# Attention of the sample tokens: value products with the probabilities as weights, and the queries' path ahead of the keys

## The chip, the cores and the metric

The kernel runs on one core of one Trainium2 chip. The metric is the device time of one execution in microseconds (us). One core has TensorE (PE, with its weight loads shown apart as PEld), VectorE (DVE), ScalarE (ACT), GpSimd (POOL) and SyncE (SP), each with a queue of its own that is worked off in order, and 16 DMA engines. The engines wait for each other by semaphores.

## The reference

One inference step through two layers, for a prompt of 256 tokens and for 8 sample tokens of 8 sequences, all in float32. Layer 0 has a recurrent branch (a gated linear recurrence over a width-4 convolution) and a differential attention with 4 heads; layer 1 has a gated delta rule and a mixture of 8 experts. The change touches the attention of layer 0:

```python
q = rmsnorm(q.reshape(B, T, H_B, 2, DH_B), g_q)          # H_B = 4, DH_B = 64
k = rmsnorm(k.reshape(B, T, H_B, 2, DH_B), g_k)
s1 = einsum('bqhd,bkhd->bhqk', q1, k1) * DH_B ** -0.5
s2 = einsum('bqhd,bkhd->bhqk', q2, k2) * DH_B ** -0.5
p = softmax(s1) - lam * softmax(s2)
o = einsum('bhqk,bkhe->bqhe', p, v)
o = rmsnorm(o, subln_g) * (1.0 - lam_init)
y = concatenate([gelu(gate) * hs, o]) @ w_out
```

For a sample token, keys and values are 256 rows of its own sequence from a paged cache (2 pages of 128 rows, 4 heads x 128 columns each) and its own new row. The normalised keys, the values, and the last state `hs` of the recurrence are outputs too.

## The kernel before

The activations stand transposed in on-chip memory: 128 channels on the partitions, T = 264 columns (256 prompt tokens, then 8 sample tokens). The weights stream through a ring of three slots. Each piece of a weight is split into a high part by ACT and a low part by DVE, and TensorE makes every dense product in three (high by high, low by high, high by low; lines 961, 965, 974). The eight banks that TensorE writes hold 512 float32 columns each.

Every engine's program is written out by hand. The tables `scalar_steps`, `tensor_steps`, `vector_steps` and `gpsimd_steps` (lines 98 to 124) name the events that share one counting semaphore for each engine; the order in the table must be the order in that engine's program. `at(name, n)` is the semaphore and the count at which the n-th event of that name has happened.

The order of the work between the input projection and the output projection `w_out_e` is this:

- TensorE spreads the queries' and keys' norm factors over the partitions (line 2122, eight products that contract over 16 rows, one for each tile of 128 channels), and DVE scales the tiles with them (line 1480). `q_done` comes after the fourth, `qk_done` after the eighth.
- TensorE turns the 8 samples' queries into rows (line 2131, bank 6). ACT copies them to `qs_tok` (line 1057), after its gelu (line 1054). TensorE then spreads one sample's query row over 128 partitions (`query_rows`, line 2126, a product of 8 rows and 512 columns), for the first two samples at once and for each further one when the sample two before it has been scored.
- TensorE turns keys, the convolution's tail and the last recurrent states into rows (lines 2139, 2142, 2146). ACT copies the first two kinds (lines 1060, 1062) and DVE the last one (line 1515), between its first two samples. The prompt's scores (lines 2159, 2160) stand between the samples' query rows.
- DVE scores each sample against its key pages: products (line 1507) and sums (line 1510). When a sample's keys are used, POOL has the next pages fetched into one of four buffers (`load_pages`, line 735): the 16 key pages first, then the 16 value pages.
- After the softmax (ACT line 1090 for the prompt, lines 1094 to 1099 for the samples, DVE lines 1519 to 1547) TensorE turns the samples' probabilities (lines 2180, 2181), and DVE copies them out (lines 1550, 1551, `pT_s`).
- For each of the four heads TensorE turns the prompt's probabilities (line 2204), makes one sample's value products (`sample_values`, line 2186) and then the prompt's value products (lines 2210 to 2212); ACT copies what comes out (lines 1106, 1108). Samples 4 to 7 follow, with the prompt's norm sums (line 2216) and the spreading of its norm factors (line 2226, 4 rows) between them.
- The first half of the first chunk of `w_out_e` (four tiles, the dense lines 961, 965, 974) has the samples' norm between its tiles (`sample_norm`, line 2230): sums after tile 0, spread factors (line 2237) after tile 2. The second half of the chunk needs the samples' columns (`mix_hi_s`, `mix_lo_s`).

One sample's value products, before:

```python
for h in range(HB):
    o = bank[7][:, h * TS + b:h * TS + b + 1]
    for g in range(NP_):
        last = PE.matmul(o, pages_kv[:, n % 4, g, h * P:(h + 1) * P], pT_s[:, g, h * TS + b:h * TS + b + 1],
                         start=g == 0, stop=g == NP_ - 1)
```

The first operand after the output is the one that is loaded as weights, the next one is streamed. So each value page is loaded as weights, one head at a time, and one column of probabilities is streamed against it. `P` is 128, `TS` 8 samples, `HB` 4 heads, `NB` = 32, `NP_` = 2 pages, `AW` = 512.

## Time and profile before

| what | value |
|---|---|
| median of 3 runs | 1780.21 us (1776.52 to 1781.13) |
| the profiled execution, its own time | 1780.29 us |
| its span, first to last instruction | 1778.5 us |
| mean granted TensorE clock | 0.949 of full |
| busy share of the span: PE, PEld, DVE, ACT, POOL | 95%, 82%, 74%, 60%, 11% |
| records of TensorE | 9601 |
| DMA | 445.49 MB, mean 250 GB/s |

A granted clock of 1.00 is 2.4 GHz and 0.50 is 1.2 GHz. A float32 product leaves two records on TensorE, each with a weight load. "Busy" counts time in which an engine had an instruction in work, at whichever clock. "Idle" time of an engine stands in brackets in the timeline, with what ended it. The chain of waits is followed back from the last instruction, at each step to what released it.

### The profile page before, as it was taken

The page shows a single profiled execution, that of the slowest core. Times are in us where ns is not written, and L with a number is a line of the kernel's source. Part 1 is how long each engine was busy: PE and PEld are TensorE (multiplying, and loading weights), DVE is VectorE, ACT ScalarE, POOL GpSimd, SP SyncE. Part 2 cuts the span into 40 slices and gives each one's busy share as a digit, 9 for nine tenths or more (in the row PEclk, how much of TensorE's full clock was granted, in tenths as well). Part 3 has the DMA queues.
Part 4 walks back from the last instruction along what each step waited for, and adds up shares of the span by engine and source line. Part 5 has one row for each costly group of instructions (what it writes and reads, how often), then busy time and mean ns, then how long its engine had stood idle before and what let it go on. Part 6 is the DMA issues. An engine that isn't in the chain of part 4 may idle for free.

```text
span 1778.5 us, 25250 instructions
## 1 busy us (share of the span) xinstructions
PE 1697.5 (95%) x9601; PEld 1466.7 (82%) x9601; DVE 1317.4 (74%) x1436; ACT 1062.7 (60%) x1052; POOL 201.4 (11%) x237
## 2 busy tenths in 40 slices
PE   8979999999888989999999999999999999999997
PEld 7848999998878986888888888888888888888885
DVE  5782455445757646578898898898888888898986
ACT  5541443335554334477777777777777776776774
POOL 5320111102247621100000000000000000000000
PEclk9965999999999985899999999999999999999999
DMA  9451344544340024479999899899899899899993
GB/s 297 162 162 58 110 175 143 196 165 144 134 132 28 2 60 140 168 282 359 341 341 378 325 343 377 319 357 375 309 364 377 308 368 376 301 372 336 347 369 122
DMA packets 199195, 445.49 MB, mean 250 GB/s; under 512 B 9569, under 2 KB 20995, under 8 KB 199071
## 3 DMA queue, kind: packets, MB, share of 16 engines
q1 hardware_dynamic: 184698, 423.88, 66.2%
q0 software_dynamic: 3968, 12.85, 2.5%
q10 hardware_dynamic: 10448, 7.65, 1.4%
q8 instruction: 55, 0.90, 0.2%
q14 instruction: 26, 0.21, 0.0%
HBM read 437.28 MB, written 7.29 MB: 250 GB/s over the span
## 4 chain that ended last, share of the span: by engine, by line
PE 85%; DVE 8%; ACT 3%; issue 2%; POOL 1%; PEld 1%; DMA 0%; PEldq 0%; DVEq 0%; ACTq 0%; SPq 0%; POOLq 0%
PE bank L2590 17%; PE bank L2569 11%; PE bank L2570 11%; PE bank L2574 11%; PE bank L961 6%; PE bank L965 5%; PE bank L974 5%; PE bank L2540 2%; PE bank L2193 1%; DVE weight_lo L552 1%; PE bank L2370 1%; PE bank L2550 1%; PE bank L2436 1%; ACT weight_hi L549 1%; PE bank L2380 1%
## 5 line engine op out<-in xcount | busy, mean ns | idle before, releaser
L552 DVE TENSOR_TENSOR weight_lo<-weight_ring,weight_hi 128x2048 fp32r<-128x2048 f32 x349 | 790.0, 2273 | 241.1 <-ACT weight_hi L549 217.6
L549 ACT ACTIVATE weight_hi<-weight_ring 128x2048 fp32r<-128x2048 f32 (+1 forms) x358 | 679.9, 1903 | 309.9 <-PE bank L974 98.8
L2569 PE MATMUL bank<-weight_hi,h_lo 128*128 128x512 f32 x896 | 354.2, 395 | 0.1
L2570 PE MATMUL bank<-weight_hi,h_hi 128*128 128x512 f32 x896 | 349.2, 390 | 0.0
L2574 PE MATMUL bank<-weight_lo,h_hi 128*128 128x512 f32 x896 | 239.8, 389 | 0.0
L2574 PEld LDWEIGHTS bank<-weight_lo,h_hi 128*128 128x128 f32 x896 | 168.2, 188 | 35.0
L2569 PEld LDWEIGHTS bank<-weight_hi,h_lo 128*128 128x128 f32 x896 | 168.3, 188 | 34.6 <-DVE h_lo L1958 0.4
L2570 PEld LDWEIGHTS bank<-weight_hi,h_hi 128*128 128x128 f32 x896 | 168.4, 188 | 33.4
L2590 PE MATMUL bank<-weight_hi,h_lo 128*128 128x512 f32 x448 | 120.6, 391 | 1.8 <-DVE h_lo L1963 1.8
L2590 PE MATMUL bank<-weight_hi,h_hi 128*128 128x512 f32 x448 | 119.8, 389 | 0.0
L2590 PE MATMUL bank<-weight_lo,h_hi 128*128 128x512 f32 x448 | 119.8, 389 | 0.0
L552 DVE TENSOR_TENSOR weight_lo<-work,weight_hi 128x2048 fp32r<-128x2048 f32 x48 | 109.8, 2287 | 12.6 <-ACT weight_hi L549 12.6
L961 PE MATMUL bank<-n_hi,weight_hi 128*128 128x264 f32 x608 | 104.6, 295 | 13.6 <-issue 4.3
L549 ACT ACTIVATE weight_hi<-work 128x2048 fp32r<-128x2048 f32 x48 | 92.1, 1919 | 26.7 <-PE bank L2574 20.3
L965 PE MATMUL bank<-n_hi,weight_lo 128*128 128x264 f32 x608 | 101.6, 290 | 4.6 <-POOL weight_lo L605 3.8
L961 PEld LDWEIGHTS bank<-n_hi,weight_hi 128*128 128x128 f32 x608 | 86.7, 194 | 18.0 <-issue 13.7
L2590 PEld LDWEIGHTS bank<-weight_hi,h_lo 128*128 128x128 f32 x448 | 83.5, 188 | 19.0 <-DVE h_lo L1963 2.1
L2590 PEld LDWEIGHTS bank<-weight_hi,h_hi 128*128 128x128 f32 x448 | 84.1, 188 | 17.6
L2590 PEld LDWEIGHTS bank<-weight_lo,h_hi 128*128 128x128 f32 x448 | 84.1, 188 | 17.5
L961 PE MATMUL bank<-h_hi,weight_hi 128*128 128x264 f32 x464 | 89.1, 297 | 2.6 <-issue 1.0
L965 PEld LDWEIGHTS bank<-n_hi,weight_lo 128*128 128x128 f32 x608 | 87.0, 195 | 5.0 <-POOL weight_lo L605 4.0
L965 PE MATMUL bank<-h_hi,weight_lo 128*128 128x264 f32 x464 | 86.3, 291 | 1.5 <-DVE weight_lo L552 1.5
(510 smaller groups left out, 2218.9 us busy)
## 6 DMA issues: line engine op xcount, KB each, us to landing
weight_ring<-in_moe_wg SPq DMA_DIRECT2D x104, 1024.0 KB, 7.1
weight_ring<-in_moe_wu SPq DMA_DIRECT2D x96, 1024.0 KB, 7.3
weight_ring<-in_moe_wd SPq DMA_DIRECT2D x88, 1024.0 KB, 6.4
work<-in_moe_wd SPq DMA_DIRECT2D x24, 1024.0 KB, 7.1
weight_ring<-in_w_in_o SPq DMA_DIRECT2D x8, 2048.0 KB, 8.7
work<-in_moe_wu SPq DMA_DIRECT2D x16, 1024.0 KB, 5.8
weight_ring<-in_ffn_wg SPq DMA_DIRECT2D x5, 2048.0 KB, 7.9
weight_ring<-in_ffn_wu SPq DMA_DIRECT2D x5, 2048.0 KB, 7.8
```

What stands on the lines that cost most here:

```text
L549: return SC.activation(whi[:, p % SPLIT, 0:size], src, ACT.Copy).then_inc(sig("hi_done"), 1)
L552: V.tensor_tensor(wlo[:, p % SPLIT, 0:size], src, whi[:, p % SPLIT, 0:size].bitcast(F32), ALU.subtract)\
L961: PE.matmul(out, hi[:, jj, cols_], a_hi[:, j0 + j, :], start=first and j == 0, stop=False)
L965: PE.matmul(out, lo[:, jj, cols_], a_hi[:, j0 + part * half + jj, :], start=False, stop=False)
L974: last = PE.matmul(out, hi[:, jj, cols_], a_lo[:, j0 + j, :], start=False, stop=last_one and j == k - 1)
L2193: last = PE.matmul(o, pages_kv[:, n % 4, g, h * P:(h + 1) * P], pT_s[:, g, h * TS + b:h * TS + b + 1], start=g == 0, stop=g == NP_ - 1)
L2370: last = PE.matmul(bank[STREAM[u]][:, k * P:(k + 1) * P], Am[:, h, :], Tt[:, h, :], start=True, stop=True)
L2540: last = PE.matmul(bank[(7, 3)[r]][:, jj * CAP:(jj + 1) * CAP], h_tok[:, i, j * P:(j + 1) * P], sel[:, i, :], start=i == 0, stop=i == NTT - 1)
L2569: PE.matmul(out, hte_l[:, j, :], hi[:, jj, :], start=j == 0, stop=False)
L2570: PE.matmul(out, hte_h[:, j, :], hi[:, jj, :], start=False, stop=False)
L2574: last = PE.matmul(out, hte_h[:, j, :], lo[:, jj, :], start=False, stop=j == KD - 1)
L2590: last = PE.matmul(bank[5 + hf][:, :], lhs[:, c % 2, k, :], rhs[:, kk, hf * CHUNK_COLS:(hf + 1) * CHUNK_COLS], start=c == 0 and k == 0 and ...
```

## The change

The change has three parts.

**The samples' value products.** The probabilities become the weights and a whole value page of 512 columns is streamed: one product for each page, of 32 weight columns. The weights `p_rows` have for each sample and page 32 columns, one for each pair of head and sample; only the four of this sample are filled, the others are zero. All 16 products of the 8 samples accumulate in one bank of 32 rows (head and sample) by 512 columns. DVE fills `p_rows` with zeros once (between its first two samples) and copies the probabilities in with one strided copy for each head. At the end DVE copies the bank out (`o_rows`), and TensorE turns each head's 8 rows back into 8 columns with a product against the identity (`os_rows_T`), ahead of the samples' norm, whose steps move by one tile.

**The queries ahead of the keys.** TensorE spreads the four query factors, turns the samples' queries (now in bank 3) as soon as they are scaled, and only then spreads the key factors; the last of these waits for ACT's copy, which now stands ahead of the gelu.

**Two steps change place or engine.** The product of gelu and recurrence (`lru_done`) and the copy of the last states (`hlast`): the first moves on DVE from before the first sample to behind it, the second from DVE to ACT.

```diff
@@ the order of events (one of four tables; the others move likewise)
-              ("qk_b", HH), ("qs_psum", 1), ("qb_first", 2), ("ktok_psum", 3), ("tail_psum", 1),
+              ("qk_b", HB), ("qs_psum", 1), ("qk_b_keys", HB), ("qb_first", 2), ("ktok_psum", 3), ("tail_psum", 1),
...
-        hl_tok = after_lru[0:TS + 1, 1100:1100 + LW]
+        hl_tok = after_lru[0:TS + 1, 1030:1030 + LW]
+        p_rows = after_lru[:, 1542:1542 + NP_ * TS * NB].rearrange("p (g c) -> p g c", g=NP_)
+        o_rows = after_lru[0:NB, 0:AW]
@@ ACT
+            act_e.wait_ge(*at("qs_psum", 1))
+            SC.activation(qs_tok, bank[3][0:TS, :], ACT.Copy).then_inc(sig("qs_tok"), 1)
             SC.activation(proj[:, GATE:GATE + NL, :], proj[:, GATE:GATE + NL, :], ACT.Gelu_apprx_tanh).then_inc(sig("gelu"), 1)
-            act_e.wait_ge(*at("qs_psum", 1))
-            SC.activation(qs_tok, bank[6][0:TS, :], ACT.Copy).then_inc(sig("qs_tok"), 1)
...
             SC.activation(tail_tok, bank[7][0:TAIL, 0:LW], ACT.Copy).then_inc(sig("tail_tok"), 1)
+            act_e.wait_ge(*at("hlast_psum", 1))
+            SC.activation(hl_tok, bank[3][0:TS + 1, 0:LW], ACT.Copy).then_inc(sig("hlast"), 1)
@@ DVE
             V.tensor_copy(hl, xc[:, :, TP - 1:T])
-            dve.wait_ge(*at("gelu", 1))
-            V.tensor_tensor(mixT[:, 0:NL, :], proj[:, GATE:GATE + NL, :], xc, ALU.mult).then_inc(sig("lru_done"), 1)
...
                 if b == 0:
-                    dve.wait_ge(*at("hlast_psum", 1))
-                    V.tensor_copy(hl_tok, bank[3][0:TS + 1, 0:LW]).then_inc(sig("hlast"), 1)
+                    dve.wait_ge(*at("gelu", 1))
+                    V.tensor_tensor(mixT[:, 0:NL, :], proj[:, GATE:GATE + NL, :], xc, ALU.mult).then_inc(sig("lru_done"), 1)
+                    link(V.memset(p_rows, 0.0))
...
-            V.tensor_copy(pT_s, bank[6][:, 0:NP_ * NB].rearrange("p (g n) -> p g n", g=NP_))
+            for h in range(HB):
+                V.tensor_copy(p_rows[:, :, h * TS:h * TS + (NB + 1) * (TS - 1) + 1:NB + 1],
+                              bank[6][:, 0:NP_ * NB].rearrange("p (g n) -> p g n", g=NP_)[:, :, h * TS:(h + 1) * TS])
...
             dve.wait_ge(*at("v_pages_used", TS))
+            V.tensor_copy(o_rows, bank[7][0:NB, :]).then_inc(sig("o_rows"), 1)
+            dve.wait_ge(*at("os_rows_T", 1))
             V.tensor_tensor(o_s, pself.rearrange("p (h b) -> p h b", h=HB),
-                            bank[7][:, 0:NB].rearrange("p (h b) -> p h b", h=HB), ALU.add).then_inc(sig("o_sample"), 1)
+                            bank[6][:, P:P + NB].rearrange("p (h b) -> p h b", h=HB), ALU.add).then_inc(sig("o_sample"), 1)
@@ TensorE
+            spread_norms(range(0, HB), "qk_b")
+            pe.wait_ge(*at("proj_done", 20))
+            pe.wait_ge(*at("q_done", 1))
+            for h in range(HB):
+                last = PE.transpose(bank[3][0:TS, h * P:(h + 1) * P], proj[:, Q_ + h, TP:T], ident[:])
+            last.then_inc(sig("qs_psum"), 1)
+            spread_norms(range(HB, 2 * HB - 1), "qk_b_keys")
+            pe.wait_ge(*at("qs_tok", 1))
+            spread_norms((2 * HB - 1,), "qk_b_keys")
...
-                for h in range(HB):
-                    o = bank[7][:, h * TS + b:h * TS + b + 1]
-                    for g in range(NP_):
-                        last = PE.matmul(o, pages_kv[:, n % 4, g, h * P:(h + 1) * P], pT_s[:, g, h * TS + b:h * TS + b + 1],
-                                         start=g == 0, stop=g == NP_ - 1)
+                for g in range(NP_):
+                    last = PE.matmul(bank[7][0:NB, :], p_rows[:, g, b * NB:(b + 1) * NB], pages_kv[:, n % 4, g, :],
+                                     start=b == 0 and g == 0, stop=b == TS - 1 and g == NP_ - 1)
                 last.then_inc(sig("v_pages_used"), 1)
...
             def sample_norm(c):
                 if c == 0:
+                    pe.wait_ge(*at("o_rows", 1))
+                    for h in range(HB):
+                        last = PE.matmul(bank[6][:, P + h * TS:P + (h + 1) * TS], o_rows[:, h * P:(h + 1) * P], ident[0:NB, h * TS:(h + 1) * TS],
+                                         start=True, stop=True)
+                    last.then_inc(sig("os_rows_T"), 1)
+                if c == 1:
                     pe.wait_ge(*at("os_sq", 1))
...
-                if c == 2:
+                if c == 3:
                     pe.wait_ge(*at("os_inv", 1))
```

`spread_norms` issues the products of line 2122 for the heads it is given. The line numbers in the rows of the changed kernel differ from those of the kernel before: 2122 is 2128 there, 2131 is 2136, 2126 is 2145, 2193 is 2205, 2204 is 2216, 2216 is 2228, 2226 is 2238, 2237 is 2255.

On TensorE, from the norm factors to the keys' rows (8x128 are the turned queries, `bank<-work,ident` the query rows, the last two rows the keys' rows), the order before was

```order
L2122 MATMUL bank<-work 128x264 x8
L2131 MATMUL bank<-ident,work 8x128 x4
L2126 MATMUL bank<-work,ident 128x512 x2
L2139 MATMUL bank<-ident,work 128x128 x8
L2139 MATMUL bank<-ident,work 8x128 x4
```

and is now

```order
L2128 MATMUL bank<-work 128x264 x4
L2136 MATMUL bank<-ident,work 8x128 x4
L2128 MATMUL bank<-work 128x264 x4
L2145 MATMUL bank<-work,ident 128x512 x2
L2153 MATMUL bank<-ident,work 128x128 x8
L2153 MATMUL bank<-ident,work 8x128 x4
```

The queries' rows now stand between the query factors and the key factors.

On DVE, from the scaling of queries and keys to the second sample (a sample is two products and two sums), the order before was

```order
L1480 SCALAR_TENSOR_TENSOR work<-work,par,bank 128x264 x8
L1485 COPY small<-work 128x36
L1487 TENSOR_TENSOR work<-work 128x1056
L1489 TENSOR_TENSOR small<-small 128x1
L1490 TENSOR_SCALAR small<-small 128x1
L1507 TENSOR_TENSOR work<-work,bank 128x512 x2
L1510 TENSOR_REDUCE hT<-work 128x4x2 x2
L1515 COPY hT<-bank 9x512
```

and is now

```order
L1483 SCALAR_TENSOR_TENSOR work<-work,par,bank 128x264 x8
L1488 COPY small<-work 128x36
L1490 TENSOR_TENSOR small<-small 128x1
L1491 TENSOR_SCALAR small<-small 128x1
L1508 TENSOR_TENSOR work<-work,bank 128x512 x2
L1511 TENSOR_REDUCE hT<-work 128x4x2 x2
L1516 TENSOR_TENSOR work<-work 128x1056
L1517 MEMSET hT 128x512
```

The product of 128x1056 moved behind the first sample, the copy of the last states left, and the fill came in.

On TensorE, from the last head to the dense products of `w_out_e` (`work,sm` the norm sums, `work,ident` the spread factors), the order before was

```order
L2193 MATMUL bank<-small,work 128x1 x8
L2216 MATMUL bank<-work,sm 4x256 x4
L2193 MATMUL bank<-small,work 128x1 x16
L2226 MATMUL bank<-work,ident 128x256 x4
L2193 MATMUL bank<-small,work 128x1 x8
L961 MATMUL bank<-h_hi,weight_hi 128x264 x4
```

and is now

```order
L2205 MATMUL bank<-work,hT 32x512 x2
L2228 MATMUL bank<-work,sm 4x256 x4
L2205 MATMUL bank<-work,hT 32x512 x4
L2238 MATMUL bank<-work,ident 128x256 x4
L2205 MATMUL bank<-work,hT 32x512 x2
L963 MATMUL bank<-h_hi,weight_hi 128x264 x4
```

Each sample's eight products have become two; their place is the same.

## Rows read from the trace of the kernel before

**Rows 1.** Chain of waits, 137 to 181 us: start, us, what, number of records.
```profile
137.67 0.90 PE bank L2204 x3
...
138.57 3.21 PE bank L2193 x16
...
141.78 0.64 PE bank L2210 x2
...
143.27 0.64 PE bank L2204 x3
...
143.91 3.21 PE bank L2193 x16
...
162.47 3.50 PE bank L2216 x8
...
165.98 6.92 PE bank L2193 x32
...
172.89 3.70 PE bank L2226 x8
...
180.10 1.09 PE bank L961 x4
```

**Rows 2.** Windows: busy us (instructions) per engine, granted clock, DMA share, GB/s.
```profile
93.20:96.60 3.40, 3.40 (x18) 2.45 (x16) 3.40 (x9) 3.37 (x3) 1.09 (x2) 1.00 0.24 69
...
103.50:106.80 3.30, 3.30 (x19) 2.27 (x17) 1.11 (x2) 1.41 (x3) 0.96 (x2) 0.50 0.50 128
...
106.90:110.20 3.30, 3.30 (x18) 1.55 (x16) 3.13 (x6) 1.75 (x5) 0.13 (x1) 1.00 0.06 24
...
137.70:180.00 42.30, 42.30 (x181) 38.40 (x181) 8.49 (x9) 7.37 (x12) 4.29 (x8) 0.50 0.18 50
...
180.00:185.30 5.30, 5.30 (x30) 5.02 (x31) 0.38 (x2) 0.49 (x2) 0.00 (x0) 0.50 0.00 0
...
411.60:417.40 5.80, 5.80 (x26) 5.80 (x27) 4.31 (x10) 4.95 (x9) 0.38 (x1) 0.50 0.73 274
...
667.00:670.00 3.00, 3.00 (x8) 0.90 (x8) 2.23 (x9) 2.97 (x9) 0.00 (x0) 0.50 0.01 3
```

**Rows 3.** Timeline, TensorE: start, us, line, out<-in, shapes, number of records.
```profile
97.42 3.77 PE L2126 MATMUL bank<-work,ident 8*128 8x512 f32 x4 [0.68 <-ACT work L1057]
...
103.74 1.06 PE L2142 MATMUL bank<-ident,work 128*11 128x128 f32 x4
...
107.70 1.12 PE L2126 MATMUL bank<-work,ident 8*128 8x512 f32 x2
...
187.26 1.05 PE L2237 MATMUL bank<-work,ident 4*128 4x8 f32 x8
...
667.08 5.08 PE L2464 MATMUL bank<-work,sm 128*8 128x256 f32 x16
```

**Rows 4.** Timeline, VectorE, in brackets its idle time before.
```profile
96.75 1.25 DVE L1487 TENSOR_TENSOR work<-work 128x1056 f32<-128x1056 f32 x1
...
105.69 0.68 DVE L1515 COPY hT<-bank 9x512 f32<-9x512 f32 x1 [3.51 <-PE bank L2146]
...
106.30 1.26 DVE L1507 TENSOR_TENSOR work<-work,bank 128x512 f32<-128x512 f32 x2
...
109.01 1.28 DVE L1507 TENSOR_TENSOR work<-work,bank 128x512 f32<-128x512 f32 x2
...
137.31 0.20 DVE L1550 COPY small<-bank 128x64 f32<-128x64 f32 x1
...
178.24 1.23 DVE L1565 TENSOR_TENSOR h_lo<-work,h_hi 128x1024 fp32r<-128x1024 f32 x1 [1.12 <-ACT h_hi L1115]
```

**Rows 5.** The page's DMA issues of the value pages: KB, us to landing.
```profile
work<-in_cache_v POOLq DMA_DIRECT2D x16, 256.0 KB, 3.0
```

**Rows 6.** Timeline, GpSimd, the first page asked for again.
```profile
142.98 0.54 POOL L739 DMA_DIRECT2D work<-in_cache_v  x1 [9.88 <-issue]
```

**Rows 7.** Timeline, ScalarE, the samples' rounded copy.
```profile
188.63 0.23 ACT L1121 ACTIVATE h_hi<-work 128x32 fp32r<-128x32 f32 x1 [5.11 <-DVE work L1574]
```

More of the change, by code:

```diff
@@ L99, in program @@
               ("norm0_hi", KD), ("norm0_sq", KD), ("lam_absexp", 1), ("lam_exp", 1), ("norm0_root", 1),
-              ("lru_gates", 2 * NL), ("lru_a", 2), ("lru_root", 1), ("qk_root", 1), ("vtok", 3), ("gelu", 1),
-              ("qs_tok", 1), ("ktok", 3), ("tail_tok", 1), ("scores_first", 4), ("ya_hi", 1), ("scores_rest", HH - 4), ("exps", 2 * HH), ("ss", 1), ("exps_s", 2),
+              ("lru_gates", 2 * NL), ("lru_a", 2), ("lru_root", 1), ("qk_root", 1), ("vtok", 3), ("qs_tok", 1), ("gelu", 1),
+              ("ktok", 3), ("tail_tok", 1), ("hlast", 1), ("scores_first", 4), ("ya_hi", 1), ("scores_rest", HH - 4), ("exps", 2 * HH), ("ss", 1), ("exps_s", 2),
               ("o_sq", 1), ("o_root", 1), ("mix_hi", 1), ("os_sq", 1), ("os_root", 1), ("mix_hi_s", 1), ("norm1_sq", KD), ("norm1_root", 1), ("ffn_sil", NF), ("wba_hi", 1),
@@ L1478, in _ @@
                 g = r_gq if i < HB else r_gk
-                dve.wait_ge(*at("qk_b", i + 1))
+                dve.wait_ge(*at("qk_b" if i < HB else "qk_b_keys", i % HB + 1))
                 last = V.scalar_tensor_tensor(proj[:, Q_ + i, :], proj[:, Q_ + i, :], par[:, g:g + 1], bank[(i + 4) % 8][:, 0:T],
@@ L2113, in _, with spread_norms @@
                      between=mid_chunk, norm=0, chunks=IN_ORDER, late=late_chunk)
+            def spread_norms(heads, done):
+                for i in heads:
+                    if i < 4:
+                        if i:
+                            pe.wait_ge(*at("vtok", i))
+                    else:
+                        pe.wait_ge(*at("proj_done", 13 + i))
+                    PE.matmul(bank[(i + 4) % 8][:, 0:T], spread[:, i * P:(i + 1) * P], inv[0:NQK, 0, :], start=True, stop=True).then_inc(sig(done), 1)
             pe.wait_ge(*at("qk_inv", 1))
             pe.wait_ge(*at("spread_made", 1))
-            for i in range(2 * HB):
-                if 1 <= i < 4:
-                    pe.wait_ge(*at("vtok", i))
-                elif i >= 4:
-                    pe.wait_ge(*at("proj_done", 13 + i))
-                PE.matmul(bank[(i + 4) % 8][:, 0:T], spread[:, i * P:(i + 1) * P], inv[0:NQK, 0, :], start=True, stop=True).then_inc(sig("qk_b"), 1)
+            spread_norms(range(0, HB), "qk_b")
[7 more added lines that the diff above has]
+            spread_norms((2 * HB - 1,), "qk_b_keys")
             def query_rows(b):
@@ L2127, in query_rows @@
                   .then_inc(sig("qb_first" if b < 2 else "qb_rest"), 1)
-            pe.wait_ge(*at("q_done", 1))
-            for h in range(HB):
-                last = PE.transpose(bank[6][0:TS, h * P:(h + 1) * P], proj[:, Q_ + h, TP:T], ident[:])
-            last.then_inc(sig("qs_psum"), 1)
-            pe.wait_ge(*at("qs_tok", 1))
             for b in range(2):
@@ L2189, in sample_values @@
                 pe.wait_ge(*at(f"kv{n % 4}_loaded", 32 * (n // 4 + 1)))
-                for h in range(HB):
-                    o = bank[7][:, h * TS + b:h * TS + b + 1]
-                    for g in range(NP_):
-                        last = PE.matmul(o, pages_kv[:, n % 4, g, h * P:(h + 1) * P], pT_s[:, g, h * TS + b:h * TS + b + 1],
-                                         start=g == 0, stop=g == NP_ - 1)
+                for g in range(NP_):
+                    last = PE.matmul(bank[7][0:NB, :], p_rows[:, g, b * NB:(b + 1) * NB], pages_kv[:, n % 4, g, :],
+                                     start=b == 0 and g == 0, stop=b == TS - 1 and g == NP_ - 1)
                 last.then_inc(sig("v_pages_used"), 1)
```

6 lines of the change are left out of this document (3 added, 3 removed).

## The prediction

> **What bounds the kernel now.** I read the chain of waits for the stretch that the change touches, then the windows with the granted clock, then the timelines. The chain from 137.67 to 180.10 us is TensorE and nothing else: 42.3 us without a gap. Head by head, three transposes of the probabilities, one sample's value products and the prompt's value products follow each other, the next sample starting 5.34 us after the last (138.57 and 143.91), and then come the other samples [rows 1]. The two samples at 165.98 took 6.92 us for 32 records (two records to a product), 0.216 us each [rows 1]. So the eight samples are 27.7 us of 42.3, for 128 records whose moving operand is one column wide.
>
> In the windows the reader should see that these 42.3 us are all "PE busy" and yet have a granted clock of 0.50, that is 1.2 GHz, and that the dense products behind them keep 0.50 for another 5.3 us [rows 2]. The clock was 1.00 (2.4 GHz) until 96.6 us, in a stretch full of the factor products of line 2122, which contract over 16 rows, and fell behind it; it came back for one stretch behind that from 103.5 to 106.8 us; and it rose some 5.4 us after the dense work began at 180 [rows 2]. At 667 us products with 128 rows, 256 columns and only 8 weight columns ran at 0.50 for 3.0 us, eight records; the other eight of the 16 took the remaining 2.1 of 5.08 us, so the clock rose behind the first eight [rows 2, 3]. Few weight columns did not keep it down there.
>
> **The change part by part. 1, value products.** 128 records of one column become 32 records (16 products) of 512 columns with 32 weight columns. Four 512-wide records took 3.77 us at a clock of 0.50, and two took 1.12 us at 1.00 [rows 3]. Less a tail of about 0.2 us at the end of each group, a record is 0.9 us at half clock and 0.46 at full; exact halves of the 0.9 give 0.45, and a record without tail subtracted 0.56. At half clock a sample is then 3.4 to 3.6 us, what it is now. So **the exchange by itself is worth nothing**; it pays only if the clock rises. I expect that: now every record from 137.7 us on is 128 to 512 columns wide, nearly all have 128 rows, and no wait lies between. It rose 3.0 us after the start of such work at 667 us, 5.4 us after it at 180, and 411.6 to 417.4 us was busy at 0.50 for 5.8 us [rows 2]. I take 5.0 us, with 3.0 and 6.8 as ends (one over the longest, whose start is blurred). What remains of the 42.3 us, 37.3, takes half: 5.0 + 18.65 = 23.65 us. One wait comes up: after the last head ACT copies and squares before the norm sums can start, which a sample of 3.4 us hid and one of 1.7 just hides; 0.2 us for it. Gain **18.4 us**.
>
> The pages don't hold this up. A sample's pages are asked for when the one four before it is used: POOL issued the first at 142.98, 1.2 us after the sample ended at 141.78 [rows 1, 6]; the second follows within 1.2 us, and 3.0 us from issue to landing [rows 5] make 5.4. At full clock over 8 us lie between the two.
>
> **2, dense work behind.** It finds the clock at 1.00. The 5.3 us at 0.50 [rows 2] become 2.7: gain **2.7 us**.
>
> **3, the samples' way in and out.** The probabilities leave their bank in four strided copies in place of one of 0.20 us [rows 4], and TensorE waits for them: three more, **+0.55 us**. Behind the products DVE copies 32x512 out of the bank (the 9x512 copy took 0.68 us), standing behind the subtraction that began at 178.24 and took 1.23 [rows 4]. That one ended 2.9 us after the spread products (172.89 + 3.70) [rows 1, 4], so the copy ends 3.6 us after them. TensorE has 1.7 us of the last sample and one dense tile left (four of its twelve records took 1.09 us at half clock [rows 1], so some 1.5 us at full) and wants the copy at 3.2: **+0.4 us**. Four products turn the rows back: eight records of the same form (128 weight columns, 8 moving) took 1.05 us at 187.26 [rows 3]: **+1.0 us**. Last, the norm factors are spread after tile 3 instead of tile 2, so the second half of the chunk stands directly behind them and waits for DVE's scaling and ACT's copy: 188.31 to 188.86 us in the old order [rows 3, 7], 0.55, with the wait's own delay **+0.6 us**. Nothing covers it any more.
>
> **4, queries ahead of keys.** TensorE spreads four query factors, waits for DVE's fourth scaling, transposes, spreads three keys, and the fourth after ACT's copy, which is now covered. One wait is exchanged for another of like size, and the key products stand later, some of them behind the fall of the clock at 96.6 us [rows 2]. The first query row was begun at 97.42 us [rows 3]; I put it at 97.5 to 98.3. On DVE the 3.51 us of idle time before the 0.68 us copy go away between the first two samples; the 1.25 us product and a fill of 512 columns (no row; between 0 and the 0.68 of that copy) come in [rows 4]. The second sample starts about 2.2 us earlier than 106.30 [rows 4]. But the third (109.01 [rows 4]) needs the row product that TensorE began at 107.70 [rows 3], behind 20 transposes and six score products that nobody shortens. So **what DVE wins it waits out again before the third sample**, and the stage ends with TensorE's delay, **+0.5 us**; ends -0.7 (no wait for ACT's copy, nothing in its place) and +1.7 (0.9 for the key products at half clock, 0.8 if the row product at 107.70 doesn't find 1.00).
>
> Sum: -18.4 - 2.7 + 0.55 + 0.4 + 1.0 + 0.6 + 0.5 = **-18.1 us**. What follows hangs on this chain and moves with it. The profiled execution took 1780.29 us, as good as the median of 1780.21: **1762.2 us**.
>
> **The rivals.** *A, the clock rises and falls once more.* The four products that spread the norm factors contract over 4 rows (3.70 us at half clock [rows 1]) and resemble what ran before the fall at 96.6. Against: they last only 1.9 us at full clock, between wide products. Price: the last sample and the first dense tiles at half clock, as now, 2.7 us: 1764.9.
>
> *B, transposes don't count for the clock.* Then the heads' part, with 0.64 us of transposes in each 5.3 [rows 1], might leave it down, and it would rise only in sample 4 and the norm sums (3.50 us [rows 1]), 6.8 us in one piece. 21.3 + 5.0 us would run at half clock, the other 16.0 in 8.0: gain 8.0 + 2.7 - 3.05 = 7.7, so 1772.6. Against it: what ran from 103.5 to 106.8 us was for the larger part transposes (four of them the row at 103.74), and 1.00 followed [rows 2, 3]. The Trainium skill (TensorE: Matmul & The Clock Gate, section "Part 4: PE-mode transpose") says that transpose mode doesn't count as busy in the way other products do. This case's trace disagrees.
>
> *C, slower: the clock stays at 1.2 GHz.* The mechanism: a product with 32 of 128 weight columns, seven in eight of its weights zero, works too little of the array. Then parts 1 and 2 give nothing and the additions stay: 0.55 + 1.7 (eight records at 0.216) + 0.6 + 0.5 = 3.4 us, so 1783.7, or 1784.9 with part 4 at its end. It has decided if the clock is still 0.50 at 146 us. Against it stands the rise behind 8 weight columns [rows 2, 3].
>
> *D, DVE's 2.2 us of part 4 are kept*, because TensorE reaches the third sample's row at full clock: 1760.
>
> **How the numbers follow.** The forecast has 0.74, A 0.12, D 0.05, B 0.04, C 0.05. The likeliest gives 1762.2. Its lower end: rise after 3.0 us (-1.0), part 4 at -0.7 (-1.2), no stalls behind the samples (-1.0), which is 1759.0, and D near it; runs lie up to 3.7 us under their median: 1757.5. Upper: rise after 6.8 (+0.9), part 4 (+1.2), some 24 wide records at 0.56 (+2.6), and rounding up to take in A with part 4's end: 1768.5. A difference of 0.3% (5.3 us) is about what a measurement of this kernel can tell from none. Faster by more than that: all but C, with something off for what I have not seen, 0.94; within it 0.04; slower by more 0.02, for C with a further wait.
>
> **What would show it.** A granted clock of 1.00 from about 143 to 145 us on; samples 1.7 to 1.8 us long; the dense work beginning near 162 us; DVE idle some 2 us before the third sample; a short idle of TensorE before the four turning products and one before the second half of the chunk. Wrong would be: 0.50 until sample 4 (B) or to the end of the samples (C), a wait for a page, or 512-wide records that stay near 0.85 us at 1.00.

## The result and the profile after

The changed kernel takes 1764.82 us (median of 4 runs, 1764.41 to 1766.85); the kernel before took 1779.52 us beside it (4 runs, 1776.52 to 1781.13). The ratio is 0.9922, 95% interval 0.9904 to 0.9939. The profiled execution took 1764.41 us, its span 1762.8 against 1778.5. The forecast was 1762.2.

From the changed kernel's page, busy time and granted clock in 40 slices:

```profile
PE 1679.5 (95%) x9513; PEld 1437.0 (82%) x9513; DVE 1320.1 (75%) x1440; ACT 1062.9 (60%) x1053; POOL 205.9 (12%) x237
...
PEclk9968999999899975999999999999999999999999
```

The windows of the changed kernel in the stretch that counts (columns as in [rows 2]):

```profile
95.60:98.00 2.40, 2.40 (x8) 1.62 (x7) 0.49 (x1) 1.63 (x2) 0.54 (x1) 0.50 0.68 142
...
109.40:112.60 3.20, 3.20 (x18) 1.43 (x15) 1.36 (x3) 1.80 (x5) 1.07 (x2) 1.00 0.32 85
...
140.10:143.40 3.30, 3.30 (x6) 1.01 (x7) 3.27 (x3) 0.49 (x1) 0.00 (x0) 0.50 0.00 0
143.40:150.00 6.60, 6.60 (x28) 2.76 (x26) 0.34 (x1) 1.64 (x4) 2.15 (x4) 1.00 0.35 91
150.00:160.00 10.00, 10.00 (x39) 3.99 (x39) 1.74 (x1) 4.00 (x6) 2.15 (x4) 1.00 0.50 152
160.00:164.70 4.70, 4.70 (x16) 1.87 (x14) 1.94 (x5) 1.06 (x1) 0.00 (x0) 1.00 0.00 0
164.70:174.20 9.50, 8.78 (x74) 8.17 (x73) 2.44 (x6) 0.90 (x4) 0.00 (x0) 1.00 0.00 0
```

In the place of 42.3 us at 0.50 there are 3.3 us at 0.50 and then 1.00 to the end. Line 2205 is a sample's value products, 2216 the transposes of the probabilities, 2222 the first of the prompt's value products, 963 the dense line that was 961. The chain of waits (start, us, what, records) shows what the clock does to a sample: 3.06 us while the clock is half for most of it, 1.83 at 1.00, where [rows 1] had 3.21:

```profile
140.07 0.90 PE bank L2216 x3
140.97 3.06 PE bank L2205 x4
144.04 0.42 PE bank L2222 x2
...
145.23 1.83 PE bank L2205 x4
...
155.82 1.73 PE bank L2228 x8
157.54 3.43 PE bank L2205 x8
160.98 1.92 PE bank L2238 x8
162.90 1.83 PE bank L2205 x4
```

In TensorE's timeline, the three places at which the change added something behind the samples:

```profile
164.66 0.77 PE L963 MATMUL bank<-h_hi,weight_hi 128*128 128x264 f32 x4
...
166.41 1.05 PE L2246 MATMUL bank<-ident,hT 32*128 32x8 f32 x8
...
172.41 1.05 PE L2255 MATMUL bank<-work,ident 4*128 4x8 f32 x8
174.16 0.72 PE L963 MATMUL bank<-h_hi,weight_hi 128*128 128x264 f32 x4 [0.70 <-ACT h_hi L1124]
```

From the starts in the timelines, part by part (before, then after):

| part | before | after | difference | forecast |
|---|---|---|---|---|
| start of the value stage | 137.67 | 140.07 | +2.40 | +1.05 |
| value stage, to the first dense product | 42.29 | 24.59 | -17.70 | -18.4 |
| dense products, to the second half of the chunk | 9.83 | 9.50 | -0.33 | -0.7 |
| the rest, to the end of the span | 1588.7 | 1588.6 | -0.1 | 0 |
| span | 1778.5 | 1762.8 | -15.7 | -18.1 |

The gain comes from where it was expected. What is dear is ahead of the stage. VectorE's timeline there:

```profile
101.87 1.28 DVE L1508 TENSOR_TENSOR work<-work,bank 128x512 f32<-128x512 f32 x2 [0.93 <-PE bank L2145]
...
105.69 0.48 DVE L1517 MEMSET hT<- 128x512 f32 x1
106.21 1.29 DVE L1508 TENSOR_TENSOR work<-work,bank 128x512 f32<-128x512 f32 x2
...
111.21 1.28 DVE L1508 TENSOR_TENSOR work<-work,bank 128x512 f32<-128x512 f32 x2 [2.40 <-PE bank L2145]
...
139.52 0.41 DVE L1553 COPY hT<-bank 128x16 f32<-128x16 f32 x4
```

The idle 2.40 us before the third sample are there as forecast, but that sample starts at 111.21, not 109.01 [rows 4]. In TensorE's timeline the first query row begins at 99.87, against 97.42 [rows 3].

### The profile page after: what moved, and what is told of

It is laid out like the page before. It is cut to its first block, busy times and chain, and to the rows that moved or that the text cites. A ratio compares the mean times of both kernels' runs of the same rounds, so it can differ in the third digit from the quotient of the medians.

```text
span 1762.8 us, 25083 instructions
## 1 busy us (share of the span) xinstructions
PE 1679.5 (95%) x9513; PEld 1437.0 (82%) x9513; DVE 1320.1 (75%) x1440; ACT 1062.9 (60%) x1053; POOL 205.9 (12%) x237
## 3 DMA queue, kind: packets, MB, share of 16 engines
q10 hardware_dynamic: 10448, 7.65, 1.4%
## 4 chain that ended last, share of the span: by engine, by line
PE 85%; DVE 7%; ACT 3%; issue 2%; PEld 1%; POOL 1%; DMA 0%; PEldq 0%; ACTq 0%; DVEq 0%; SPq 0%
PE bank L2608 17%; PE bank L2587 12%; PE bank L2588 12%; PE bank L2592 12%; PE bank L963 6%; PE bank L967 5%; PE bank L976 5%; PE bank L2558 2%; DVE weight_lo L554 2%; PE bank L2568 1%; PE bank L2388 1%; ACT weight_hi L551 1%; PE bank L2454 1%; PE bank L2398 1%; PE bank L2401 1%
```

## Experiments

Each group of four had its own runs of the kernel before; their medians were 1780.94 (e1 to e4), 1782.71 (e5 to e8) and 1784.30 us (e9 to e12), so ratios compare better than times across groups. The readings of all profiled executions stand first, since most verdicts use them. The clock's falls and rises are from windows of 0.2 us; the others are starts in TensorE's and VectorE's timelines.

| kernel | clock, 90 to 190 us | first query row | fourth sample (DVE) | value stage, length | second half begins | rest of span |
|---|---|---|---|---|---|---|
| before | down 96.8, up 107.0, down 110.4, up 185.4 | 97.42 | 111.74 | 137.67, 42.29 | 189.79 | 1588.7 |
| after | down 95.8, up 109.4, down 112.8, up 143.6 | 99.87 | 113.94 | 140.07, 24.59 | 174.16 | 1588.6 |
| e5 (after again) | down 97.8, up 104.6, down 114.8, up 142.0 | 97.81 | 110.58 | 136.69, 25.51 | 171.69 | 1591.1 |
| e1 values only | down 94.8, up 108.4, down 115.2, up 142.6 | 99.26 | 113.23 | 139.36, 24.45 | 173.30 | 1589.0 |
| e2 queries only | down 95.6, up 105.8, down 116.0, up 184.2 | 99.02 | 111.79 | 137.75, 42.29 | 189.27 | 1590.0 |
| e3 rows 128 | down 114.6, up 138.4 | 97.59 | 108.51 | 134.65, 24.79 | 168.92 | 1589.4 |
| e9 (e3 again) | down 115.2, up 139.0 | 97.13 | 108.06 | 134.20, 25.26 | 168.94 | 1592.1 |
| e10 factors only | down 107.2, up 138.0 | 97.42 | 108.44 | 134.57, 24.56 | 168.62 | 1589.7 |
| e4 filler | down 97.8, up 104.6, down 114.8, up 128.4, down 135.4, up 142.2 | 98.02 | 110.70 | 136.85, 25.45 | 171.80 | 1589.8 |
| e6 tile 2 | down 96.8, up 107.0, down 113.8, up 141.2 | 97.97 | 111.80 | 137.93, 24.46 | 171.25 | 1590.6 |
| e7 held | no fall | 97.00 | 107.92 | 134.05, 23.01 | 166.56 | 1589.2 |
| e12 all | down 117.8, up 121.2 | 97.40 | 108.32 | 134.44, 23.00 | 166.29 | 1593.8 |
| e8 held, old values | down 116.8, up 120.2, down 140.6, up 174.8 | 97.36 | 108.23 | 134.16, 36.47 | 179.84 | 1590.1 |
| e11 before, rows 128 | down 113.0, up 164.2, down 167.6, up 177.8 | 97.36 | 107.61 | 135.76, 39.17 | 183.72 | 1589.8 |

The last column is work that no edit touches, and it takes 1588.6 to 1593.8 us. A term under 2 us is therefore read from the stage that it is in, and not from a median of four runs.

**e1_values_only: the query part undone.** Order of factors, query transposes and ACT's copies as before; value products as changed.

```diff
-            spread_norms(range(0, HB), "qk_b")
...
-            spread_norms(range(HB, 2 * HB - 1), "qk_b_keys")
-            pe.wait_ge(*at("qs_tok", 1))
-            spread_norms((2 * HB - 1,), "qk_b_keys")
+            for i in range(2 * HB):
...
+                PE.matmul(bank[(i + 4) % 8][:, 0:T], spread[:, i * P:(i + 1) * P], inv[0:NQK, 0, :], start=True, stop=True).then_inc(sig("qk_b"), 1)
```

> The change with its query part undone: TensorE spreads all eight factors first and turns the queries behind them, ACT's gelu stands ahead of the queries' copy. In the changed kernel the third sample starts on DVE 1.9 us later than before (111.21 against 109.01, less 0.3 us by which everything stood later). Theory: that is the price of the queries ahead of the keys; without it the third sample starts near 109.3 us and the time is 1762.9 us, 1.9 under the changed kernel. Rival: the delay comes from the new order on DVE (product and fill between the first two samples) or from where the clock happened to fall; then this kernel stays within 0.5 us of the changed one, 1764.8.

Measured: 1764.68 us (5 runs), ratio 0.9914 (0.9898 to 0.9930): the same as the changed kernel. The rival's number came. Here too the first query row is late (99.26), in the old order, with the clock falling at 94.8: a delay of this size comes without the new order as well.

**e2_queries_only: the value part undone.** The kernel before, with the query part of the change.

```diff
-            for i in range(2 * HB):
...
+            spread_norms(range(0, HB), "qk_b")
...
+            spread_norms(range(HB, 2 * HB - 1), "qk_b_keys")
```

> The change with its value part undone: value products with the pages as weights as before, no fill, no turning back, norm steps at their old tiles; the queries ahead of the keys and the moved copies stay. Theory: all of the gain is the value side's, and the queries' side costs 1.5 to 2 us: 1781 to 1781.5 us, granted clock 0.50 to the end of the samples. Rival: the queries' side wins by itself what DVE no longer waits (2 us): 1777.5.

Measured: 1779.41 us (12 runs), ratio 0.9997 (0.9988 to 1.0006). Neither number: no gain or loss of the reordering shows, within 0.12%. The second sample starts at 104.71 instead of 106.30, VectorE then idles 1.76 us before the third, and the fourth starts at 111.79, against 111.74. What VectorE wins is waited out, as forecast, and no price is left: the first query row stands 1.60 us later than before (99.02 against 97.42), the fourth sample 0.05.

**e3_rows128: products over all 128 rows.** The eight factor products contracted over 16 rows, the query rows over 8. Here both run over 128; the added rows of the weights are zeros.

```diff
-        spread = kt_flat[0:NQK, 0:2 * HB * P]
+        spread = kt_flat[:, 0:2 * HB * P]
-                    PE.matmul(bank[(i + 4) % 8][:, 0:T], spread[:, i * P:(i + 1) * P], inv[0:NQK, 0, :], start=True, stop=True).then_inc(sig(done), 1)
+                    PE.matmul(bank[(i + 4) % 8][:, 0:T], spread[:, i * P:(i + 1) * P], inv[:, 0, :], start=True, stop=True).then_inc(sig(done), 1)
-                PE.matmul(bank[4 + b % 2][:, 0:AW], ident[0:TS, b:b + 1].broadcast_to([TS, P]), qs_tok, start=True, stop=True)\
+                PE.matmul(bank[4 + b % 2][:, 0:AW], ident[:, b:b + 1].broadcast_to([P, P]), inv_flat[:, 1024:1024 + AW], start=True, stop=True)\
```

> The changed kernel, with the norm factors and the samples' query rows spread by products that contract over all 128 rows instead of 16 and 8; the added rows meet zero weights, so the result is the same and the number and width of the products too. Theory: the clock falls at 95.6 us because TensorE then works with few rows; with 128 rows it stays at 1.00 until DVE alone sets the pace, the key factors take 0.23 us a record instead of 0.44, the first query rows 0.43 instead of 0.85, the keys' and states' rows half; the first sample starts near 98.5 us instead of 101.9 and the third is no longer waited for: 5 to 7 us less, 1758 to 1760. Rival: rows don't matter, it was the wait for DVE before the queries that let the clock fall: within 0.5 us of 1764.8 and the same fall.

Measured: 1760.10 us (4 runs), ratio 0.9888 (0.9869 to 0.9906). The theory held in place, and in time but for 0.1: 4.7 us less than the changed kernel's 1764.8, where 5 to 7 were expected. The clock fell only at 114.6, when TensorE waited for VectorE's samples. In e3's timeline the same products, 128 rows deep:

```profile
95.80 1.95 PE L2128 MATMUL bank<-work 128*128 128x264 f32 x8
97.59 1.88 PE L2145 MATMUL bank<-work,ident 128*128 128x512 f32 x4
```

In the changed kernel, at half clock, they were

```profile
96.19 3.88 PE L2128 MATMUL bank<-work 16*128 16x264 f32 x8
99.87 3.62 PE L2145 MATMUL bank<-work,ident 8*128 8x512 f32 x4
```

and e3's windows have the clock at 1.00 through all of it:

```profile
97.50:101.00 3.50, 3.50 (x22) 2.25 (x20) 3.35 (x9) 2.59 (x5) 0.00 (x0) 1.00 0.23 70
101.00:106.00 5.00, 3.69 (x26) 2.09 (x26) 4.74 (x8) 2.80 (x7) 1.07 (x2) 1.00 0.34 85
```

**e4_filler: six filler products before the value stage.** Three stand before the wait for the last scores and three before that for the probabilities, each 128x512, with a result that nobody reads.

```diff
+            pe.wait_ge(*at("tail_tok", 1))
+            for _ in range(3):
+                PE.matmul(bank[7][:, :], ident[:], proj.rearrange("p a b -> p (a b)")[:, Q_ * T:Q_ * T + CHUNK_COLS], start=True, stop=True)
...
+            for _ in range(3):
+                PE.matmul(bank[7][:, :], ident[:], proj.rearrange("p a b -> p (a b)")[:, Q_ * T:Q_ * T + CHUNK_COLS], start=True, stop=True)
             pe.wait_ge(*at("p_s", 1))
```

> The changed kernel, with three products of 128 rows and 512 columns (identity against the queries, into a bank that nobody reads before it is cleared) behind the last query row and three more before TensorE waits for the samples' probabilities. Theory: the first 3.3 us of the value stage (140.07 to 143.36) run at 0.50 only because TensorE stood idle before; with the filler the stage begins at 1.00 and is 1.6 us shorter, 1763.2 us. Rival: the clock falls again in the pauses that stay, or the filler itself stands in the way of the scores' transposes: 1764.8 to 1766.

Measured: 1763.28 us (5 runs), ratio 0.9908 (0.9892 to 0.9923). The theory's time came, but not by its mechanism. The windows of e4:

```profile
128.40:132.80 4.40, 4.18 (x14) 1.50 (x12) 4.26 (x17) 0.86 (x4) 1.61 (x3) 1.00 0.59 180
132.80:135.40 2.60, 0.29 (x4) 0.29 (x3) 2.50 (x10) 0.93 (x4) 0.00 (x0) 0.96 0.32 102
135.40:136.80 1.40, 0.51 (x3) 0.37 (x2) 1.40 (x8) 0.00 (x0) 0.00 (x0) 0.50 0.00 0
136.90:142.20 5.30, 5.30 (x12) 1.95 (x13) 3.59 (x3) 0.49 (x1) 0.00 (x0) 0.52 0.00 0
```

The fillers raised the clock; at 135.2, 0.1 us behind the end of the pause of 2.31 us that followed them, it fell again, and the stage began at 0.50 as ever. Against the changed kernel's own profile the execution gained because the clock fell later around 97 us, long before the fillers ran. Nor is the median apart from the changed kernel's: the intervals of e4, of e5 and of the first measurement overlap. The expected number came without the expected cause.

**e5_after_again: the changed kernel once more.**

> The changed kernel once more, unaltered, as the control of this group. Expected 1764.8 us as before, within 1764 to 1767. If the place at which the clock falls around 95 us wanders from execution to execution, the profile shows the fall anywhere from 94.8 to 97.8 us and the start of the value stage between 139 and 141 us; if it is fixed by the code, 95.8 and 140.1 again.

Measured: 1763.96 us (4 runs), ratio 0.9899 (0.9883 to 0.9914). The median is as expected (0.04 under the stated range). The fall wandered, to 97.8 us, with nothing edited, and the stage began at 136.69: 3.4 us before that of the other profile, and 2.3 before the earliest that was stated. Its first 5.3 us then ran at 0.50 (rise 142.0), where the other execution had 3.3. Two executions of one kernel thus differ by +3.4 and -0.9 us in two neighbouring stages.

**e6_factors_tile2: norm factors behind tile 2.**

```diff
-                if c == 3:
+                if c == 2:
                     pe.wait_ge(*at("os_inv", 1))
```

> The norm factors are spread behind dense tile 2 instead of tile 3. In the changed kernel TensorE waits 0.70 us for ACT before the second half of the chunk, with tile 3 (about 1.6 us) standing ahead of the factors. Theory: tile 3 then covers that wait, and TensorE finds os_inv ready behind tile 2: stage from the first dense product to part 2 of 8.8 instead of 9.5 us, 1764.1 us in all, and no idle time before part 2. Rival: DVE's sums and reciprocal are not ready behind tile 2, TensorE waits for os_inv instead, and the stage keeps its 9.5 us: 1764.8.

Measured: 1765.50 us (5 runs), ratio 0.9913 (0.9900 to 0.9927). The timeline shows the theory's 0.64 us (8.86 from the first dense product to the second half, against 9.50) and no idle time in front of it:

```profile
168.69 1.05 PE L2255 MATMUL bank<-work,ident 4*128 4x8 f32 x8
169.67 0.76 PE L963 MATMUL bank<-h_hi,weight_hi 128*128 128x264 f32 x4
...
171.25 0.65 PE L963 MATMUL bank<-h_hi,weight_hi 128*128 128x264 f32 x4
```

The median doesn't: it is 1.5 us above e5's, and both ratios' intervals overlap. The wait is gone; that the kernel is faster for it is not shown.

**e7_clock_held: no fall at all.** e3's edit and 18 fillers in the waits between the samples.

```diff
+                for _ in range({5: 3, 6: 1, 7: 6}.get(b, 0)):
+                    PE.matmul(bank[7][:, :], ident[:], proj.rearrange("p a b -> p (a b)")[:, Q_ * T:Q_ * T + CHUNK_COLS], start=True, stop=True)
...
+            for _ in range(5):
+                PE.matmul(bank[7][:, :], ident[:], proj.rearrange("p a b -> p (a b)")[:, Q_ * T:Q_ * T + CHUNK_COLS], start=True, stop=True)
             pe.wait_ge(*at("p_s", 1))
+            for _ in range(1):
+                PE.matmul(bank[7][:, :], ident[:], proj.rearrange("p a b -> p (a b)")[:, Q_ * T:Q_ * T + CHUNK_COLS], start=True, stop=True)
```

> The factor and query-row products over 128 rows as in e3_rows128, and 18 filler products of 512 columns in the waits between the samples (3, 1 and 6 behind the query rows 5, 6 and 7, 5 before the wait for the scores, 1 before that for the probabilities). Theory: the clock stays at 1.00 from the first sample to the value stage; the stage, which in e3 spent its first 3.7 us at half clock, begins at 1.00 and takes 21.5 to 22.5 us instead of 24.79; 1757.5 to 1758.5 us. Rival: as in e4_filler the clock falls in one of the waits all the same, or the fillers stand in the way: 24.8 us again and 1760 or more.

Measured: 1758.94 us (4 runs), ratio 0.9872 (0.9857 to 0.9887). The windows of e7:

```profile
97.00:120.00 23.00, 17.67 (x77) 8.74 (x76) 20.74 (x36) 13.13 (x32) 7.90 (x14) 1.00 0.54 162
120.00:134.00 14.00, 12.40 (x35) 5.08 (x34) 13.52 (x40) 5.62 (x25) 3.23 (x6) 1.00 0.48 134
134.05:157.06 23.01, 23.01 (x85) 9.25 (x85) 7.27 (x9) 7.20 (x12) 4.30 (x8) 1.00 0.32 92
```

The clock is held in this execution, and the stage is 23.01 us, the whole of it at 1.00 and without a pause. That is 1.8 us under e3, not the 2.3 to 3.3 expected; an earlier rise can give no more. The time of 1758.9 lies 0.4 above the expected range. The same fillers did not always hold the clock: in the profiles of e8 and e12 it fell for 3.4 us, at 116.8 and 117.8, and was back before the stage.

**e8_held_old_values: e7 with the one-column value products of before.**

```diff
-                for g in range(NP_):
-                    last = PE.matmul(bank[7][0:NB, :], p_rows[:, g, b * NB:(b + 1) * NB], pages_kv[:, n % 4, g, :],
-                                     start=b == 0 and g == 0, stop=b == TS - 1 and g == NP_ - 1)
+                for h in range(HB):
+                    o = bank[7][:, h * TS + b:h * TS + b + 1]
+                    for g in range(NP_):
+                        last = PE.matmul(o, pages_kv[:, n % 4, g, h * P:(h + 1) * P], pT_s[:, g, h * TS + b:h * TS + b + 1],
+                                         start=g == 0, stop=g == NP_ - 1)
```

> The same as e7_clock_held, but with the value products of before: 128 records of one column, with the values as weights, and no turning back. It asks whether the wide products pay by themselves or by the clock. Theory: by the clock alone. The stage begins at 1.00, the one-column products let it fall within 3 to 8 us, and from there on a sample takes its old 3.4 us and a head its 5.3: stage of 38 to 41 us, 1772 to 1776 us in all, clock at 0.50 from about 140 us to the dense work. Rival: a clock that is already at 1.00 stays there with one-column products also (0.122 us a record at 1.00 by the row at 670 us): the stage takes about 25 us or less and the total is that of e7 within 3 us, 1757 to 1761 us; then the width itself was never needed.

Measured: 1770.33 us (4 runs, 1763.38 to 1771.65), ratio 0.9921 (0.9899 to 0.9942). The chain of waits of e8:

```profile
134.71 1.68 PE bank L2209 x16
136.39 0.33 PE bank L2226 x2
...
137.50 1.68 PE bank L2209 x16
...
140.28 2.83 PE bank L2209 x16
143.11 0.64 PE bank L2226 x2
...
145.24 3.20 PE bank L2209 x16
```

and of e7, with the wide products:

```profile
134.60 1.83 PE bank L2212 x4
136.43 0.42 PE bank L2229 x2
...
137.63 1.83 PE bank L2212 x4
```

This is the experiment that says what the width is for. At 1.00 a sample of one-column products takes 1.68 us, less than the 1.83 of the wide ones; a head takes 2.79 us (134.71 to 137.50) against 3.03 (134.60 to 137.63). But 6.4 us into the stage, at 140.6, the clock fell, with TensorE 100% busy all the while, and a sample was back at 3.20 us. The theory held in kind and not in size: the stage took 36.47 us and not 38 to 41, the time lies 1.7 under the expected 1772 to 1776, and one run of the four was as fast as 1763.38; where the clock fell in it isn't known, for it has no trace. Against e7 (0.9872, 0.9857 to 0.9887) the intervals are apart.

**e9_rows128_again** (e3's kernel) was the control of the last group.

> The kernel of e3_rows128 once more, as the control of this group: 1760 us, within 1759 to 1762. Clock at 1.00 through the factor products and query rows, with the fall behind them at about 115 us; the value stage of 24 to 25.5 us begins at half clock.

Measured: 1761.53 us (4 runs), ratio 0.9874 (0.9857 to 0.9890), as expected.

**e10_factors_only: e3 without the query rows.** Only the factor products run over 128 rows.

> Only the factor products of line 2128 over 128 rows instead of 16; the query-row products keep their 8 rows. Theory: the factor products, which run back to back before the clock falls, decide it; the clock is then still at 1.00 when the first query row is spread, and the value stage begins near 135 us; 1760 to 1761 us, as e9. Rival: products with 8 rows are enough to let it fall; the clock goes at some place between 97 and 110 us and the gain is half or less: 1762 to 1764 us.

Measured: 1763.11 us, ratio 0.9890 (0.9871 to 0.9909), from four runs of 1759.97, 1760.80, 1765.41 and 1766.36. The profiled one, 1759.97, has its first query row at 97.42 and its stage at 134.57, as e3. But its clock fell at 107.2, without a pause of TensorE since 102.45, where e3 still had 1.00: the rival's fall, in the stretch that the rival named, though without the rival's price, for the stage began as early as e3's. For this execution the factor products alone decide when the stage starts. The median, 1763.11, lies in the rival's range and not in the theory's; what the clock did in the two slower runs isn't known, and it stays open.

**e11_before_rows128: e3's edits in the kernel before.**

> The kernel before, with the two edits of e3_rows128 and nothing of the change. Theory: the rows decide the clock before the samples whatever the order of the queries and keys, and the one-column products let it fall in the value stage: the stage begins near 135 us, its first heads may run at 1.00 (as in e8), the rest at 0.50: 40 to 42.3 us long; in all 4 to 7 us under the before of this group, a ratio of 0.996 to 0.998. Rival: with the clock raised ahead of the stage the old products keep it, and the ratio falls to 0.990 or less.

Measured: 1774.70 us (4 runs), ratio 0.9951 (0.9931 to 0.9970). That is 9.6 us under the before of its group, more than the 4 to 7 of the theory, and short of the rival's 0.990. The profile is 6.1 us ahead of before at the second half of the chunk (183.72 against 189.79); 1.9 of them come before the stage. No head ran at 1.00, which the theory had allowed for; all ran at 0.50. And then, by the windows,

```profile
160.50:164.00 3.50, 3.50 (x10) 0.85 (x9) 0.00 (x0) 0.00 (x0) 0.00 (x0) 0.50 0.03 11
164.00:167.60 3.60, 3.60 (x33) 3.60 (x32) 1.74 (x1) 0.47 (x1) 0.00 (x0) 0.97 0.00 0
167.80:171.50 3.70, 3.70 (x10) 2.48 (x9) 1.44 (x3) 0.00 (x0) 0.00 (x0) 0.50 0.00 0
```

the norm sums (256 columns wide, only 4 weight columns) were followed by a clock of 1.00, and the 32 one-column records behind them, 100% busy, by its fall. That makes 3.1 us in the stage (39.17 against 42.29, where 40 to 42.3 were expected); the last 1.0 is in the dense products, in which the clock rose 2.9 us after their start and not 5.4.

**e12_all: e7 with the factors behind tile 2.** The edits are those of e6 and e7.

> The changed kernel with everything that held: factor and query rows over 128 rows, the 18 fillers of e7_clock_held, and the norm factors behind tile 2 as in e6_factors_tile2. Theory: the parts add up: 1.2 us under e9 for the fillers (1760.1 against 1758.9 in two groups) and 0.65 for the factors: 1758.2 us, within 1757 to 1760; ratio near 0.987. Rival: the fillers' gain is within the scatter and is given back by longer waits between the samples: 1760, the same as e9.

Measured: 1759.82 us (4 runs), ratio 0.9862 (0.9846 to 0.9879). Inside the theory's range, 1.6 us over its figure and 1.7 under e9. Up to the second half of the chunk its profile is the earliest of all (166.29, e9's 168.94), but its rest took 1593.8 us, the longest of all. It beats both the kernel before and the changed one (0.9862 against 0.9922 and 0.9899, intervals apart); against e7 and e9 the intervals overlap.

## Why the prediction was right, and where its steps were off

The forecast's case came: the clock rose early in the value stage and stayed. The time, 1764.8 for 1762.2, is inside the range, and 2.6 us over. By the spans it is 2.4 (15.7 for 18.1): 1.35 of them ahead of the value stage, 0.7 in it and 0.4 in the dense products behind it. Step by step:

- **"The exchange by itself is worth nothing"** nearly held at half clock. A wide sample took 3.4 to 3.6 us, as forecast, in e5's first head (chain of waits):

```profile
137.59 3.55 PE bank L2205 x4
```

The old one took 3.21 in the heads [rows 1], not the 3.46 that the pair at 165.98 gave. At full clock the exchange costs 0.24 us in each of the four heads, 1.0 in all (e8 against e7), and the forecast had nothing for it. For the other four samples no cost is shown: the wide pair of the changed kernel took 3.43 us, and a pair with one column 3.80 in e11, at 1.00 but for some 0.4 us (timeline; the next products start at 167.79):

```profile
163.99 3.87 PE L2193 MATMUL bank<-small,work 128*128 128x1 f32 x32
```

- **The rise** came 3.3 us after the stage began, and 5.3 us after in e5, against 5.0 taken and 3.0 and 6.8 as ends. The later it is, the longer the stage (24.59 and 25.51).
- **"What remains takes half"**: 39.0 us of old work went into 21.3, not 19.5. Inside the stage this term was most out, and e7, at 1.00 throughout, shows where it goes: its heads took 3.03 us each, half of the old 5.34 is 2.67. Of the 0.36 between them 0.24 is the width; the other 0.12 is that old products, too, take more than half at 1.00 (e8's head 2.79, its sample 1.68 against 3.21). Four heads make 1.4 us of it; the rest, some 0.4, is not assigned. Against it stood an earlier rise, (5.0 - 3.3) / 2 = 0.85, and the wait of 0.2 before the norm sums, which did not come. So errors of +1.8 and -1.05 left 17.70 where 18.4 was put down: that the stage came out so near is partly luck.
- **The dense work** gained less than 2.7 from the clock: 9.50 less 1.05 for turning back, 0.70 idle and some 0.1 of waiting for VectorE's copy is 7.65, 2.2 under the old 9.83. Here too old work did not halve: four dense records took 0.88 us at 0.50 and 0.48 at 1.00, and the eight of the samples' norm sums 0.28 at either. Turning back was 1.05 (forecast 1.0), the wait behind the norm factors 0.70 (0.6), that for the copy 0.1 (0.4): the copy began at 165.68, when the first tile was nearly through.
- **The four copies of the probabilities** took 0.41 us together, where the one before took 0.20 [rows 4]: +0.2 on the path, not +0.55.
- **The step that failed is part 4's +0.5.** It treated the fall at 96.6 us as fixed and asked how the new order would lie beside it. Half of its mechanism was right: two profiles in which the clock fell at 96.8 and rose at 107.0, before and e6, have the first query row at 97.42 and 97.97 (in the forecast's 97.5 to 98.3) and the fourth sample at 111.74 and 111.80: VectorE's gain is waited out. But TensorE's delay of 0.55 does not reach the samples either, and the stage, which was to end with it, starts at 137.93 against 137.67, with 0.2 of that from the copies. And the fall wanders, from 94.8 to 97.8 us between executions of kernels whose products around it are alike, and the first query row goes with it, 99.26 to 97.81; in the changed kernel's own profile it was 99.87, 1.6 past the forecast's end. That moved the stage's start to 140.07 in one profile and to 136.69 in the next. The order costs nothing that e1 and e2 could show.
- **The range.** Its terms add up to 1759.0 and 1766.9; the stated ends, 1757.5 and 1768.5, are rounded outward by some 1.5 us each. The measured time is inside either.

Of the rivals, A (a new fall at the 4-row products) is refuted: 1.00 through the row at 160.98. So is B: the clock rose in the heads' part, in e3, e5 and after, a ninth of which is transposes (0.33 of 3.03 us). The stronger case is e5, whose clock was 0.50 from 97.8 and 1.00 from 104.6 on; between them TensorE had spread query rows over 8 rows (line 2145) and then nothing but transposes (lines 2153 and 2156):

```profile
97.81 3.62 PE L2145 MATMUL bank<-work,ident 8*128 8x512 f32 x4
101.35 2.82 PE L2153 MATMUL bank<-ident,work 128*128 128x128 f32 x12
103.97 0.84 PE L2156 MATMUL bank<-ident,work 128*11 128x128 f32 x4
```

The rule of the Trainium skill (TensorE: Matmul & The Clock Gate, section "Part 4: PE-mode transpose") that the forecast weighed was not borne out in any profile here. C, that 32 weight columns with mostly zeros work too little of the array, is refuted by the same profiles, in which those products ran at 1.00. D needs VectorE's gain kept; it idled 2.40 us instead. No page was waited for.

What isn't settled: what in detail sets the moment of the fall, why e10 has two pairs of times, and why the same fillers held the clock in e7's profile and not in those of e8 and e12.

## What to carry to other kernels

A TensorE that is "100% busy" may be so at half its clock: read the granted clock of every stretch before pricing an instruction in it, and ask which products stand before each fall. Here it fell behind two kinds with no pause before the fall: products with one moving column (e8, e11), and products that contract over 16 rows (before and e1; in the changed kernel a wait of 0.68 us lay between). Whether 8 rows do the same by themselves rests on e10 against e3 alone. With the first kind made wide and the second padded with zeros to 128 rows these falls did not come, and the padding cost no time (the first eight factor records took 2.02 us in e3 and 2.01 in e5, both at 1.00). And where an edit's worth is below what executions differ by, measure it in its own stage, in more than one profile.

## What the runs showed of the hardware

- With the contraction padded with zeros the clock stayed at 1.00 (e3, e9: no fall until 114.6 and 115.2, in a wait of TensorE; in the changed kernel it fell at 95.8 and 97.8), and the value stage started 5.4 and 2.5 us earlier.
- One-column float32 products, 128 rows by 128 weight columns, ran at 0.105 us a record at 1.00 (1.68 us for 16) and were followed by a fall of the clock in e8 (at 140.6) and in e11 (at 167.6), each time with no idle time before it. The 512-column record took 0.457 us at 1.00 and 0.89 at 0.50.
- Behind products with 4 weight columns and 128 rows the clock rose (e11's norm sums, 1.00 from 164.2), and through those with 32 it stayed at 1.00 (the stage of e7).
- In e5 the clock rose at 104.6 behind transposes alone, 3.2 us of them.
- In e4 the clock that the fillers had raised fell at 135.2 us, right behind the pause of 2.31 us (to 135.11) that followed them.
- The moment of the fall differed by 2.0 us between two executions of the changed kernel (95.8 and 97.8), the value stage's start by 3.4, and the stage itself, longer by 0.9 in the earlier one, gave back part of it.
